# Expert weights and diagonals of a retrieval layer by half rows of eight, with U and V gathers alternating by half rows

## What is computed

```
cand = v1[..., :, None] + v2[..., None, :]          # 16 x 16 candidates
top_s, top_pos = lax.top_k(cand, 16)                # per token and head
expert = take_along_axis(cand_idx, top_pos)
gate = softmax(top_s)
u = take(peer_u, expert); act = gelu(einsum('chkd,cd->chk', u, zc))
v = take(peer_v, expert); w = gate * act
out = einsum('chk,chkd->cd', w, v)
```

## Time and profile before

| | |
|---|---|
| median of 3 runs | 2703.51 us (2700.43 to 2706.43) |
| span of the profiled execution | 2709.9 us |
| busy in it: PE, DVE, ACT, POOL | 83%, 56%, 26%, 29% |
| U and V gathers | 73728 packets, 536.90 MB, 48.5% of 16 DMA engines' span |
| retrieval stage | from the first gather at 1313.8 us to the end |
| V gathers | 256, issued from 1377.2 to 2687.7 us |

### The profile page before, as it was taken

One profiled execution on the slowest core, in us unless ns is written; L12 is line 12 of the kernel. 1 busy time (PEld: TensorE's weight loads), 2 busy tenths in 40 slices (PEclk: granted clock), 3 DMA queues, 4 the chain that ended last, 5 costly groups with the idle time before them and its releaser, 6 DMA issues.

```text
span 2709.9 us, 33160 instructions
## 1 busy us (share of the span) xinstructions
PE 2261.4 (83%) x12242; PEld 1658.2 (61%) x12242; DVE 1526.4 (56%) x2176; ACT 694.3 (26%) x1151; POOL 783.3 (29%) x650
## 2 busy tenths in 40 slices
PE   7899999999999999899846687776776767776668
PEld 7899999998999989899822232222232222322223
DVE  4435655543555687746765556655455555555552
ACT  5325444543344345435200000000000000000001
POOL 2000000000000443020264445544454444444451
PEclk9989999998999999999978899998998889999999
DMA  7624444353657545464499999999999999999996
GB/s 231 192 94 141 154 140 140 124 179 118 214 176 239 159 142 164 139 211 154 171 379 391 423 388 402 405 405 400 410 403 396 387 390 422 400 386 401 390 420 252
DMA packets 288435, 754.10 MB, mean 278 GB/s; under 512 B 20401, under 2 KB 221521, under 8 KB 221522
## 3 DMA queue, kind: packets, MB, share of 16 engines
q0 software_dynamic: 73728, 536.90, 48.5%
q1 hardware_dynamic: 205794, 213.71, 24.7%
q10 hardware_dynamic: 8816, 2.23, 0.5%
HBM read 750.70 MB, written 2.10 MB: 278 GB/s over the span
## 4 chain that ended last, share of the span: by engine, by line
PE 59%; DMA 23%; issue 7%; DVE 7%; ACT 1%; POOL 1%; ACTq 1%; DVEq 0%; POOLq 0%; SPq 0%
PE PS L1545 38%; DMA EX<-in_peer_v,idx 21%; PE PS L1857 14%; DMA RAW<-in_peer_u,idx 2%; DVE EX L1486 2%; PE PS L1600 1%; DVE WL L995 1%; PE PS L1673 1%; PE PS L1651 1%; POOL RAW L589 0%; DVE XL L1005 0%; PE PS L1661 0%; PE PS L1774 0%; ACTq L695 0%; PE PS L1729 0%
## 5 line engine op out<-in xcount | busy, mean ns | idle before, releaser
L1857 PE MATMUL PS<-EX,RK 128*128 128x512 f32 x2048 | 960.0, 621 | 395.5 <-ACT RK L974 208.1
L1857 PEld LDWEIGHTS PS<-EX,RK 128*128 128x128 f32 x2048 | 391.3, 198 | 963.5 <-issue 898.3
L1545 PE MATMUL PS<-XH,WH 128*128 128x256 f32 x3024 | 841.5, 287 | 22.5 <-DVE WL L995 18.8
L1545 PE MATMUL PS<-XH,WL 128*128 128x256 f32 x3024 | 834.3, 284 | 0.0
L1486 DVE CUSTOM_DVE_ANT_0 EX<-RAW,RZ 128x2048 f32<-128x2048 f32 x256 | 582.5, 2291 | 447.1 <-DMA RAW<-in_peer_u,idx 420.1
L1545 PE MATMUL PS<-XL,WH 128*128 128x256 f32 x3024 | 763.6, 284 | 5.1 <-DVE XL L1005 3.1
L995 DVE TENSOR_TENSOR WL<-RAW,WH 128x1024 fp32r<-128x1024 f32 x380 | 479.6, 1274 | 433.5 <-ACT WH L637 430.9
L1545 PEld LDWEIGHTS PS<-XH,WH 128*128 128x128 f32 x3024 | 584.2, 193 | 27.0 <-issue 21.0
L1545 PEld LDWEIGHTS PS<-XH,WL 128*128 128x128 f32 x3024 | 584.2, 193 | 0.0
L637 ACT ACTIVATE WH<-RAW 128x1024 fp32r<-128x1024 f32 x380 | 399.8, 1058 | 599.2 <-PE PS L1545 586.7
L1545 PEld LDWEIGHTS PS<-XL,WH 128*128 128x128 f32 x3024 | 542.0, 193 | 5.9 <-DVE XL L1005 3.5
(11 more groups left out here) (310 smaller groups left out, 1178.8 us busy)
## 6 DMA issues: line engine op xcount, KB each, us to landing
RAW<-in_w_in SPq DMA_DIRECT2D x110, 1024.0 KB, 5.0
RAW<-in_w_out SPq DMA_DIRECT2D x32, 1024.0 KB, 5.6
RAW<-in_w_ple_gate SPq DMA_DIRECT2D x16, 1024.0 KB, 5.7
RAW<-in_peer_wq SPq DMA_DIRECT2D x16, 1024.0 KB, 5.7
RAW<-in_w_up_a SPq DMA_DIRECT2D x8, 1024.0 KB, 5.6
RAW<-in_w_up_b SPq DMA_DIRECT2D x8, 1024.0 KB, 5.6
RAW<-in_peer_u,idx POOLq DMA_INDIRECT x256, 12.2
EX<-in_peer_v,idx POOLq DMA_INDIRECT x256, 12.7
```

The source lines that it names most:

```text
L1545: ins = mm(o[:, t, :], w[:, q, k, c], x[:, n, :], start=(begins and k == t == m == 0), stop=(ends and k == QUARTER_KT - 1 and m == len(pai ...
L1857: ins = mm(bank(4 * hf + c), diag[:, s, :], vbuf[s][:, 512 * c:512 * (c + 1)], start=False, stop=True, skip_group_check=True)
```

## The change

A row is cut in two half rows of eight experts. The weights are made once the first eight dots of a row are there, and once more after the other eight (`weigh`); ACT makes a Tanh and eight diagonals for each half; and POOL gathers V of the first half of a row between U of its second half, and V of the second half between U of the next row's first half. Ahead of the first V there are eight U in place of sixteen, and behind the last U eight V. The number of gathers, of dots, of diagonals and of matmuls is the same, and so are the buffers. The softmax's reciprocal is still made once a row.

```
+HALF_K = TOPK // 2
...
             def gather_row(r, par, last=False):
-                for k in range(TOPK + LAG):
-                    if k < TOPK:
+                for k in range(HALF_K + LAG):
+                    if k < HALF_K:
                         gather(peer_v, vbuf, v_landed, v_free, r, par, k)
+                    if k >= LAG:
+                        gather_u(r, par, HALF_K + k - LAG)
+                for k in range(HALF_K + LAG):
+                    if k < HALF_K:
+                        gather(peer_v, vbuf, v_landed, v_free, r, par, HALF_K + k)
                     if k >= LAG and not last:
                         gather_u(r + 1, 1 - par, k - LAG)
 
-            for k in range(TOPK):
+            for k in range(HALF_K):
...
-                        a.wait_ge(S["inner_ready"], r + 1)
-                        a.activation(ath[:, par, :], ain[:, par, :], ACT.Tanh, scale=GELU_S * GELU_C).then_inc(S["gel_done"], 1)
-                        a.wait_ge(S["w_ready"], r + 1)
                         for k in range(TOPK):
-                            s = k % 4
+                            s, part = k % 4, k // HALF_K
+                            if k % HALF_K == 0:
+                                cols = slice(k, k + HALF_K)
+                                a.wait_ge(S["inner_ready"], r * 2 + (part + 1))
+                                a.activation(ath[:, par, cols], ain[:, par, cols], ACT.Tanh, scale=GELU_S * GELU_C)\
+                                    .then_inc(S["gel_done"], 1)
+                                a.wait_ge(S["w_ready"], r * 2 + (part + 1))
...
+            def weigh(r, par, part):
+
+                cols = slice(part * HALF_K, (part + 1) * HALF_K)
+                v.wait_ge(u_free[3], r * 4 + (2 * part + 3))
+                v.tensor_tensor(asq[:, cols], act[:, par, cols], act[:, par, cols], ALU.mult).then_inc(S["gel_step"], 1)
+                v.wait_ge(S["gel_step"], r * 5 + (3 * part + 1))
+                v.scalar_tensor_tensor(ain[:, par, cols], asq[:, cols], 1.0 / GELU_C, act[:, par, cols], op0=ALU.add, op1=ALU.mult)\
+                    .then_inc(S["inner_ready"], 1)
+                if part == 0:
+                    v.wait_ge(S["ex_done"], r + 1)
+                    v.reciprocal(er[:, par:par + 1], es[:, par:par + 1]).then_inc(S["gel_step"], 1)
+                    v.wait_ge(S["gel_step"], r * 5 + 2)
+                v.scalar_tensor_tensor(agx[:, par, cols], act[:, par, cols], er[:, par:par + 1], eg[:, par, cols], op0=ALU.mult, op1=ALU.mult)\
+                    .then_inc(S["gel_step"], 1)
+                v.wait_ge(S["gel_step"], r * 5 + (2 * part + 3))
+                v.wait_ge(S["gel_done"], r * 2 + (part + 1))
+                v.scalar_tensor_tensor(wk[:, par, cols], ath[:, par, cols], 1.0, agx[:, par, cols], op0=ALU.add, op1=ALU.mult)\
+                    .then_inc(S["w_ready"], 1)
...
-                        v.wait_ge(u_free[3], r * 4 + 5)
...
+                            if k == HALF_K - 1:
+                                weigh(r, par, 0)
+                        weigh(r, par, 1)
 
                         v.wait_ge(S["sc_evac"], PEER_HEADS)
                         choose(r + 2, par, r * CHOOSE + 2 * CHOOSE)
```

More of the change, by code:

```diff
@@ L1487, in _ @@
                                                    op0=ALU.mult, op1=ALU.add, accum_out=act[:, par, k:k + 1]).then_inc(u_free[s], 1)
-                        v.wait_ge(u_free[3], r * 4 + 5)
-                        v.tensor_tensor(asq[:], act[:, par, :], act[:, par, :], ALU.mult).then_inc(S["gel_step"], 1)
-                        v.wait_ge(S["gel_step"], r * 3 + 1)
-                        v.scalar_tensor_tensor(ain[:, par, :], asq[:], 1.0 / GELU_C, act[:, par, :], op0=ALU.add, op1=ALU.mult)\
-                            .then_inc(S["inner_ready"], 1)
-                        v.wait_ge(S["ex_done"], r + 1)
-                        v.reciprocal(er[:, par:par + 1], es[:, par:par + 1]).then_inc(S["gel_step"], 1)
-                        v.wait_ge(S["gel_step"], r * 3 + 2)
-                        v.scalar_tensor_tensor(agx[:, par, :], act[:, par, :], er[:, par:par + 1], eg[:, par, :], op0=ALU.mult, op1=ALU.mult)\
-                            .then_inc(S["gel_step"], 1)
-                        v.wait_ge(S["gel_step"], r * 3 + 3)
-                        v.wait_ge(S["gel_done"], r + 1)
-                        v.scalar_tensor_tensor(wk[:, par, :], ath[:, par, :], 1.0, agx[:, par, :], op0=ALU.add, op1=ALU.mult)\
-                            .then_inc(S["w_ready"], 1)
+                            if k == HALF_K - 1:
+                                weigh(r, par, 0)
+                        weigh(r, par, 1)
                         v.wait_ge(S["sc_evac"], PEER_HEADS)
```

## The result

| | before | after |
|---|---|---|
| median | 2704.58 us (2700.43 to 2706.43) | 2725.35 us (2722.00 to 2728.76) |
| ratio | | 1.0075, interval 1.0062 to 1.0088 |
| span of the profiled execution | 2709.9 us | 2720.3 us |
| mean granted PE clock in it | 0.945 | 0.921 |

The changed kernel is slower, by 20.8 us in the medians (16.8 to 23.8 by the interval). A run's time is 1.7 us more than its span.

The account below looks back on a forecast made before the run. Gathers were taken to bound the expert stage, with losses at row boundaries. Start 1362.9, half rows 640.2 + 679.7 and tail 39.2 gave 2722.0 us, 12.1 over the 2709.9 span; 2703.5 + 12.1 = 2715.6, range 2684 to 2752.

Parts of the forecast that it names:

- the place of the first weights: Row 0 gathers only eight U before its first weights, which should start at 1362.9 us in place of 1387.0.
- the copy's wait: DVE's wait at copying the next row's indices until PE finishes the previous row's V, 60.1 us in all, should go.
- the much slower rival: At a half row's end U 5 to 7 land 3.10 us apart, not 2.485: 2773 us; chance 0.12.
- the faster one: Rival: gathers restart quickly at each boundary, half rows take 41.2 us and the median is 2673 us; chance 0.22.
- W: Start of a row's or half row's weights on DVE, forecast 3.08 us behind the start of the last U's dot.
- the quick restart after the first weights: Best restart in the trace before, 30.7 us from the first weights to the dot of U 4; most took over 31.
- The ends: Gains forecast at the stage's start, 24 us, and behind its last weights, 27.5 us, leaving a tail of 39.2 us.
- P: Time of a half row from one weights start to the next: 42.68 us at row ends, 42.48 in mid-row; break-even 42.19.
- The clock: PE restarts at a lower clock after boundary pauses, first V 5.15 us against 3.43; taken as already inside the half-row time.
- The small things: Four more DVE operations of about 0.17 us and one more ACT Tanh per row, all taken as beside the path.
- The third effect: Choosing the next row's experts, 13 us on DVE, follows only every second boundary: mid-row boundaries 0.2 us shorter.

Follow-up runs that it names:

- two kernels with zeros on whole rows: The kernel before with ten, then twelve, matmuls of zeros on PE ahead of each row's first V: 2693.58 us and 2678.05 us.
- both halves at the end: Kernel before, its gather order kept, with halved weights both made behind a row's last dot and the second Tanh ahead of the fifth diagonal: 2704.39 us.
- The copy of indices: Kernel before with one line moved, copying the next row's indices before the dot of k = 15 in place of k = 12: 2696.18 us.
- kernel with constant diagonals: Changed kernel with diagonals made of the constant 0.5, without the Tanh or use of the experts' weights: 2687.34 us.
- zeros ahead of V 0: Changed kernel with ten matmuls of zeros on PE ahead of each half row's first V: 2661.08 us, ratio 0.9837.
- the finer weights: Kernel before, its gather order kept, with halved weights, the first made behind the twelfth dot, second Tanh ahead of the fifth diagonal: 2672.35 us.

## Why the prediction was right or wrong

**The direction and the shape: right.** Forecast 2715.6, within 2684 to 2752, slower likeliest; measured 2725.35. Of the forecast's signs all came but one, the place of the first weights (next paragraph): 32 starts of the weights, the last at 2681.1; 42.65 us apart, the ones in the middle of a row shorter (42.59 and 42.71, for 42.48 and 42.68); the copy's wait gone; PE's wait for diagonals 330.7 us in 31 pauses and a first one, that for V 64.3; a tail of 39.2 us, as worked out, with PE busy 29.2 us in it. The dots of U 4 to U 7 are 2.49 us apart, so the much slower rival is out. So is the faster one: V 4 is issued at W + 7.49, exactly as before, from W to the dot of U 4 it takes 32.1 us in the mean of both kernels, and the quick restart after the first weights (30.7) was the exception that the text took it for.

**The ends: right.** The first weights start at 1359.0, not 1362.9. In the four experiments with the same start they lie at 1363.2, 1364.6, 1364.3 and 1361.1, about the forecast, and nothing that the change touches lies before the dot of U 7, so 1359.0 belongs to this one execution. The changed kernel's profile is some 3 us short for that, as its run is (2722.00, the lowest of four).

**What was mis-sized: the baseline that the sum was set against.** Within the profiles the sum held: 42.58 us forecast in the mean, 42.65 measured, and 2722.0 us of span against 2723.7 in the median run (2725.35 less 1.7). Of the error of 9.8 us, 8.1 came in with the last step, "the profiled execution is 6.4 us above the median of 2703.5, so the forecast is 2703.5 + 12.1". It takes the loss from an execution of before that was 7.0 us of span longer than the median run (2709.9 for 2704.6 - 1.7; set against like, the 6.4 us would be 8.1). That the forecast still came within 10 us was luck in part.

An estimate shows it. If the start (1387.0) and the tail (66.7) of before are kept, the row of its median run is (2704.6 - 1.7 - 1387.0 - 66.7) / 15 = 83.28 us in place of 83.75, and a half row of the changed kernel's median run is (2725.35 - 1.7 - 1362.9 - 39.2) / 31 = 42.63. By the working of P, row - 48.53 + 7.46 less 0.1 for the choice, a row of 83.28 gives 42.1, 0.5 us too little 31 times, 16 us: from a median execution the forecast would have been about 5 us over before, not 21.

The estimate is rough: in the profiles of the other kernels with whole rows the first weights start between 1383.2 and 1389.0, which moves the 0.5 us by 0.25 either way. Of it, 0.1 to 0.2 us may be the steady part: from the dot of U 4 to that of U 15 it takes 48.35 and 48.44 us in the two kernels with zeros on whole rows, whose profiles lie within 1 us of their medians, for 48.53 here. The rest stays open. Long executions tend to have a lower mean clock (the slowest of eleven runs with both halves at the end, 2712.42, has 0.943 for 0.946 to 0.949 in the others, and the profile of before 0.945), but no run shows that the clock causes the length. The copy of indices fits the estimate: its row of 82.70 is 1.05 us under 83.75, which would be 15.8 us, but 0.58 under 83.28, which would be 8.7; measured were 8.2.

**Why PE stands: half wrong.** The text says that V 4 waits for V 0 and V 0 for the weights. The kernel with constant diagonals shows the second link to be worth 1.3 us of the boundary. The three kernels on half rows with U ahead fit one relation to 0.2 us, half row = (V 4 behind W) + 35.1 us:

| | V 4 at W + | half row |
|---|---|---|
| changed kernel | 7.49 | 42.65 |
| no weights | 6.03 | 41.35 |
| zeros ahead of V 0 | 5.58 | 40.72 |

35.1 us is 24.6 from that issue to the dot of U 4, 7.47 to U 7 and 3.08 to the weights. So the release of V 0's buffer does set the half row, as the argument had it, but it is set in its turn by the clock (1.9 us by the zeros), the weights (about 1.3), and the place of V 0 behind four U, for which PE stands 8.67 us with no weights to wait for.

**The clock: in P, but more of it than shown.** The row read for the restart, 5.15 us for the first V, was nearly the best of its kind (5.14); over the fifteen restarts of before it was 5.93 in the mean, up to 6.74. The 3.43 us beside it is the pace from V to V; from start to release a V at full clock takes 3.73. Its cost was inside P, so the sum did not suffer. The Trainium skill (TensorE: Matmul & The Clock Gate, HAM oscillation) says that work after each such wait runs at half clock, each time round the loop. The trace agrees in part: every restart behind a pause of 8 us or more was slow, five came near the full 6.87 us that the prediction worked out by the rule (6.71 to 6.80), and the mean is 2.2 us over the 3.73 of a restart at full clock. It was the largest price that a run took away: the zeros bring 64 us back.

**The small things.** The added Tanh, the four operations on DVE and the extra chain were taken as nothing; the kernel with both halves at the end gives 0.9995 (0.9985 to 1.0004). The third effect, the choice behind every second boundary only, is 0.12 us for the 0.2 forecast, little beside the 41.2 to 44.1 us over which single half rows spread.

## What to carry to other kernels

Making a dependency finer can pay by itself and still lose if the loop is cut into as many bursts: here the finer weights gained 33 us, and the order of the gathers that came with them turned it into a loss of 21. Count how often an engine drains and restarts per unit of work, price one restart at the clock that is granted after it and against how many transfers are queued then, and look whether the wait's named cause is the last of several (take it away: if the next one ends 1.2 us earlier, it was worth 1.2). When a lead of one stream over another is taken away, ask what it was hiding: here a 13 us block on DVE, which in four pieces hid itself.

## What the runs showed of the hardware

- After 8.75 us of zeros on whole rows a pause of 2.41 us was followed by windows at 0.83 and 0.74; with a pause of 1.36 us on half rows, or 0.70 behind 10.46 us of zeros on whole rows, they stayed at 1.00. In the two kernels with ten zeros and the one with twelve, every first V behind a pause of 0.70 to 1.79 us was released in 3.73 us. Behind 1.94 to 2.85 us it went either way, more often slow (17 restarts of 5.2 to 5.4 us, four of 3.73); the same length of pause gave both.
- Zeros on PE that nobody waits for took nothing from the gathers: the DMA rate in the windows beside them was 416 to 428 GB/s.
- A gather's issue on POOL takes 0.94 us alone. One that starts while a dot runs on DVE ends 0.8 us behind that dot's end, in the changed kernel 189 times of 190 from the first weights on. Two of them (DVE, then POOL: start, us):

```profile
1989.65 2.29 DVE L1515 CUSTOM_DVE_ANT_0 EX<-RAW,RZ 128x2048 f32<-128x2048 f32 x1 [0.19 <-DMA RAW<-in_peer_u,idx]
...
1992.27 2.29 DVE L1515 CUSTOM_DVE_ANT_0 EX<-RAW,RZ 128x2048 f32<-128x2048 f32 x1 [0.32 <-DMA RAW<-in_peer_u,idx]
```
```profile
1990.57 2.18 POOL L590 DMA_INDIRECT EX<-in_peer_v,idx  x1 [0.31 <-issue]
1993.06 2.31 POOL L590 DMA_INDIRECT EX<-in_peer_v,idx  x1 [0.30 <-issue]
```

  The dots end at 1991.94 and 1994.56, the issues at 1992.75 and 1995.37. By the Trainium skill (SBUF — State Buffer, SBUF: two separate sides) a DVE instruction with two SBUF inputs and a GpSimd one that reads SBUF take the same pair of ports in turn, whole instruction by whole instruction; the dot has two such inputs (`RAW` and `RZ`), and these rows agree for the gather, which waits for the dot. The other way round is not seen: 85 dots start inside a gather's issue, and neither dot (2.29 to 2.31 us) nor issue (0.94) is longer. At the boundaries the third and fourth V and the U behind them go out every 2.5 us, about the pace at which they are transferred, so the queue doesn't get longer there.
